# Merging the even layer's norm, projection, convolution and state space scan into lanes

## The reference, cut to what matters

```
z, xbc, dt_raw, q, k, v = split_cols(h @ w_in, EVEN_SPLITS)      # 1024, 2048, 16, 1024, 1024, 1024 columns
xbc = silu(causal_depthwise_conv(xbc, conv_w, conv_b))           # 4 taps along the tokens
xs, Bs, Cs = split_cols(xbc, (1024, 512, 512))
dt = softplus(dt_raw + dt_bias);  A = -exp(A_log)
y = ssd_chunked(xs, dt, A, Bs, Cs)                               # 4 chunks of 128 tokens, 16 heads
y = rms_norm((y + xs * D_skip) * silu(z), norm_w)
y_diff = diff_attention(q, k, v, lam, subln_w, rel_bias, layer_idx)
return concatenate([y, y_diff], axis=-1) @ w_out
```

## Time and profile before

| | us |
|---|---|
| median of 3 runs | 4740.59 |
| lowest, highest | 4728.93, 4744.25 |
| the profiled execution | 4736.4 |
| its span on the core | 4734.6 |
| PE busy | 3818.8 (81%) |
| DVE busy | 1866.7 (39%) |
| ACT busy | 1363.8 (29%) |
| POOL busy | 427.2 (9%) |

### The profile page before, as it was taken

The page is one execution under the profiler, slowest core; times in us unless marked ns, Lnnn a source line. Parts: engine busy times, 40 slices in busy tenths (PEclk is TensorE's granted clock), DMA queues, the critical chain, the costliest instruction groups (busy, mean ns, idle before and its releaser), DMA issues. The chain is left out here.

```text
span 4734.6 us, 51470 instructions
## 1 busy us (share of the span) xinstructions
PE 3818.8 (81%) x19565; PEld 2909.3 (61%) x19565; DVE 1866.7 (39%) x3013; ACT 1363.8 (29%) x2134; POOL 427.2 (9%) x403
## 2 busy tenths in 40 slices
PE   4494597779998768799789888799858988879976
PEld 4374474558766645587566744687646764468764
DVE  6534424433323233323244244344335424435433
ACT  0121323332223133322242144233324213433322
POOL 0000201002000020110003200011000310001000
PEclk5596797889999977899889886899979988789988
DMA  7520030122203101213021001231113100022220
GB/s 285 185 96 1 0 107 1 71 71 71 107 36 107 36 0 54 89 54 124 32 82 42 20 1 36 71 102 67 58 46 90 33 20 1 36 89 89 71 84 27
DMA packets 201721, 306.84 MB, mean 65 GB/s; under 512 B 12213, under 2 KB 119614, under 8 KB 201278
## 3 DMA queue, kind: packets, MB, share of 16 engines
q1 hardware_dynamic: 201534, 304.25, 18.9%
HBM read 302.12 MB, written 2.11 MB: 64 GB/s over the span
## 5 line engine op out<-in xcount | busy, mean ns | idle before, releaser
L364 DVE TENSOR_TENSOR w_lo<-ring,w_hi 128x1024 fp32r<-128x1024 f32 (+1 forms) x506 | 577.9, 1149 | 1219.2 <-ACT w_hi L359 1214.7
L359 ACT ACTIVATE w_hi<-ring 128x1024 fp32r<-128x1024 f32 (+1 forms) x506 | 491.6, 975 | 1379.9 <-PE out L375 689.8
L373 PE MATMUL out<-h_lo,w_hi 128*128 128x512 f32 x1760 | 698.8, 397 | 130.3 <-DVE w_lo L364 130.3
L374 PE MATMUL out<-h_hi,w_hi 128*128 128x512 f32 x1760 | 697.1, 396 | 0.0
L375 PE MATMUL out<-h_hi,w_lo 128*128 128x512 f32 x1760 | 696.3, 396 | 0.0
L373 PE MATMUL y<-h_lo,w_hi 128*128 128x512 f32 x1248 | 500.8, 401 | 114.7 <-DVE w_lo L364 114.7
L374 PE MATMUL y<-h_hi,w_hi 128*128 128x512 f32 x1248 | 498.4, 399 | 0.0
L375 PE MATMUL y<-h_hi,w_lo 128*128 128x512 f32 x1248 | 497.9, 399 | 0.0
L373 PEld LDWEIGHTS out<-h_lo,w_hi 128*128 128x128 f32 x1760 | 334.7, 190 | 211.2 <-issue 135.4
L374 PEld LDWEIGHTS out<-h_hi,w_hi 128*128 128x128 f32 x1760 | 334.8, 190 | 75.8
L375 PEld LDWEIGHTS out<-h_hi,w_lo 128*128 128x128 f32 x1760 | 334.5, 190 | 76.2
(11 more groups left out here) (507 smaller groups left out, 5353.8 us busy)
## 6 DMA issues: line engine op xcount, KB each, us to landing
ring<-in_mlp_w SPq DMA_DIRECT2D x28, 2048.0 KB, 8.2
ring<-in_mod_w SPq DMA_DIRECT2D x24, 2048.0 KB, 8.0
ring<-in_w_up SPq DMA_DIRECT2D x40, 1024.0 KB, 7.5
ring<-in_w_in SPq DMA_DIRECT2D x22, 1024.0 KB, 5.2
ring<-in_e_w_in SPq DMA_DIRECT2D x10, 2048.0 KB, 8.3
ring<-in_w_down SPq DMA_DIRECT2D x20, 1024.0 KB, 5.0
ring<-in_o_w_in SPq DMA_DIRECT2D x6, 2048.0 KB, 8.3
ring<-in_mlp_w SPq DMA_DIRECT2D x16, 512.0 KB, 5.3
```

Of the source, the lines that this page charges most:

```text
L359: return nc.scalar.activation(hi.bitcast(F32R), x, ACT.Copy)
L364: return nc.vector.tensor_tensor(lo.bitcast(F32R), x, hi, ALU.subtract)
L373: nc.tensor.matmul(out, wh, xl, start=start, stop=False, **kw)
L374: nc.tensor.matmul(out, wh, xh, start=False, stop=False, **kw)
```

## The change

The even layer is rewritten in the second mixer's form. `norm_lane`, `Item` and `items_lane` move up in the file and are extended: a shift in the norm, items that use two weight parts, items with a function (SiLU) on the way out, items narrower than 128 columns ("few"), and a bias for the convolution's SiLU. New are `ssd_steps_lane` and `scan_lane`. `even_mixer` takes the place of `pre_norm(k, 0)`, `even_ssd` and `even_diff`:

```diff
-        relative_bias(k, a)
-        pre_norm(k, 0)
-        with k.sbuf("mixT", [P, 16, S]) as mixT:
-            even_ssd(k, a, mixT)
-            even_diff(k, a, mixT)
-            down_project(k, a["e_w_out"][0], mixT, 4, post=lambda f: k.post_gain[:, 0, f:f + 1])
+        even_mixer(k, a)
...
+            ring = r.sbuf("ring", [P, SLOTS, DT, P])
+            w_hi, w_lo = r.sbuf("w_hi", [P, DT, 4 * P]), r.sbuf("w_lo", [P, DT, 4 * P])
+            item_banks, banks = r.psum("item_banks", [P, 2, S]), r.psum("scan_banks", [P, 6, S])
+
+            BEGIN = 16.0
+            ranges = [[(col + t * P, P if n > 1 else SSD_HEADS)] for col, n in ((E_Z, 8), (E_DT, 1), (E_XBC, XBC_T), (E_Q, HEADS), (E_K, HEADS))
+                      for t in range(n)]
+            items = [Item("rows", 2 * t, 0, 2 * P, z[:, c:c + 2, t * 2 * P:(t + 1) * 2 * P], (c, c + 1), func=ACT.Silu)
+                     for t in range(4) for c in (0, 2)]
+            items += [Item("few", 8, 0, SSD_HEADS, dt_t[0:SSD_HEADS, :])]
+            items += [Item("conv", 9 + j, 0, P, xbc[:, j, :], tile=j) for j in range(XBC_T)]
+            scan_from = len(items)
+            items += [Item("feat", 25 + j, 0, P, qT[:, j, :], scale=64 ** -0.5) for j in range(HEADS)]
+            items += [Item("feat", 33 + j, 0, P, kT[:, j, :]) for j in range(HEADS)]
+            at = BEGIN
+            for m, item in enumerate(items):
+                item.begin, item.length = at, 5.6 if m < scan_from else 8.6
+                at += item.length
...
+            begin = items[scan_from].begin + 3.6
+            settle = r.lane(begin - 0.1, 0.0)
+            ROUND = 34.0
...
+        relative_bias(k, a)
+        with k.sbuf("v_rows", [P, TC, D]) as v_rows, k.sbuf("lam_cols", [P, 2]) as lam_cols:
+            neg_lam, out_gain = lam_cols[:, 0:1], lam_cols[:, 1:2]
+            project(k, [run(2, weight_tiles(w, E_V), lambda e, t, j, ps: copy_out(nc, e, v_rows[:, j, bass.ds(t * COLS, COLS)], ps), rows=True)])
+            lambda_stage(k, a, neg_lam, out_gain)
+            diff_attention(k, qT, kT, v_rows, neg_lam, out_gain, qT, 0)
+        down_project(k, a["e_w_out"][0], (xbc, qT), 4, post=lambda f: k.post_gain[:, 0, f:f + 1])
```

In the scan the weights of a chunk (`weights`, the decays inside it) are kept for two groups of heads instead of four, the 16 matmuls of L881 become four with 512 columns, the xc copy and the POOL copies of the decays go, the SiLU of z is done when z leaves PSUM, and the loop is written out:

```diff
+                nc.tensor.matmul(banks[:, 4 + g % 2, :], k.at["after"], steps[:, g % 2, :, :], start=True, stop=True).then_inc(seg_done, 1)
...
+                if c * G + g >= 2:
+                    act.wait_ge(diag_done, c * G + g - 1)
+                nc.scalar.activation(weights[:, g % 2, :, :], banks[:, 4 + g % 2, :].rearrange("p (r n) -> p r n", r=R), ACT.Exp).then_inc(exp_done, 1)
```

SBUF is needed for the region, so `band` is no longer held: `relative_bias` runs after the region, stores the band in memory and waits for that, and the odd mixer loads it again beside its table:

```diff
+            sp.wait_ge(band_out, 4)
+            sp.dma_start(k.band_rows, k.band[:, :, :]).then_inc(band_kept, 16)
+            sp.wait_ge(band_kept, 16)
...
                         sp.dma_start(table[:, :], a["ret_table"]).then_inc(table_in, 16)
-                        sp.wait_ge(table_in, 16)
+                        sp.dma_start(k.band[:, :, :], k.band_rows).then_inc(table_in, 16)
+                        sp.wait_ge(table_in, 32)
```

More of the change, by code:

```diff
@@ L632, in weight_tiles, with norm_lane @@
     return lambda t: v[:, :, bass.ds(t * COLS + col, COLS)]
-def conv_silu(k, raw, n_tiles, taps, width, tap_col, bias_col):
+def norm_lane(k, r, lane, gain, hT, log_ms, rstd, stat, shift=None):
     nc = k.nc
[L641 to L674, removed]
-                else:
-                    step = nc.scalar.activation(out, acc[:, u, :], ACT.Silu, bias=bias_col(t))
-                step.then_inc(silu_done, 1)
-            pairs(act, n_tiles, finish)
-            nc.scalar.preload_act_table_set(EXP_LN_SET)
@@ L687, in ssd_steps, with ssd_steps_lane @@
+def ssd_steps_lane(k, r, early, lane, a, decays, rows, tmp, dt_t, stat, dt_ready):
     nc = k.nc
@@ L944, in even_ssd @@
[L944 to L959 removed]
+    dt, dt_a, eacs, to_end, total = (decays[:, i, :] for i in range(5))
@@ new lines, in _ @@
+    @lane.tensor
+    def _(pe):
+        pe.wait_ge(*dt_ready)
+        for c in range(TC):
+            last = nc.tensor.transpose(stat[:, c * H:(c + 1) * H], dt_t[0:H, c * P:(c + 1) * P], k.at["ident"][0:H, 0:H])
+        last.then_inc(turn_done, 1)
+        yield 0.75
+        pe.wait_ge(step, 9)
+        for i, m in enumerate((k.at["upto"], k.at["after"], k.at["ones"])):
+            last = nc.tensor.matmul(stat[:, (i + 1) * n:(i + 2) * n], m, dt_a, start=True, stop=True)
+        last.then_inc(sum_done, 1)
@@ new lines, in _ @@
+    @lane.scalar
+    def _(act):
+        act.wait_ge(rows_in, 48)
+        nc.scalar.activation(k.ssd_d, rows[:, 2, :], ACT.Copy).then_inc(d_copied, 1)
+        nc.scalar.activation(neg[:, 0:H], rows[:, 1, :], ACT.Exp).then_inc(neg_a, 1)
+        yield 0.2
+        act.wait_ge(step, 2)
+        nc.scalar.activation(u, mag, ACT.Exp, scale=-1.0).then_inc(exp_done, 1)
+        act.wait_ge(step, 3)
+        nc.scalar.activation(mag, w1, ACT.Ln).then_inc(log_done, 1)
+        yield 0.9
+        act.wait_ge(sum_done, 1)
+        for i, out in enumerate((eacs, to_end, total)):
+            nc.scalar.activation(out, stat[:, (i + 1) * n:(i + 2) * n], ACT.Exp).then_inc(steps_ready, 1)
```

872 lines of the change are left out of this document (437 added, 435 removed).

## The result

The changed kernel took **4583.8 us** (median of 4 runs, 4574.7 to 4586.4), the kernel before, on the same chip, 4738.7 us (median of 4, 4728.9 to 4744.3). The ratio is 0.9672, with a 95% interval of 0.9650 to 0.9694: 155 us less. The forecast was 4623 us with a range from 4595 to 4660.

The account below looks back on a forecast made before the run. Outside PE-bound projections, norm, step sizes, convolution and scan leave PE idle or slow. Region 345.5 + 18.9 + 5.4 + 55.3 = 425.1 for 545.5 us: -120.4, +3 reload, -117; 4740.6 - 117 = 4623 us, range 4595 to 4660.

Parts of the forecast that it names:

- scan beside q and k: Scan with the remaining 15.5 items: 157 us of PE, 9 us idle, 2 us tail, 168 us before the barrier.
- reload of the band in the odd layer: Odd layer: the band's reload queues behind a table and is waited for, +3 us, bounds 0 and 5.4.
- everything else: SiLU of z, dropped copies of decays and quarter-size loads priced at nothing; no term for stages outside the change.
- step-size stall: Step sizes: PE waits 5 us with the sums of the decays, bounds 1 and 12 us.
- The two ends: Rivals: q and k stand behind the scan, 4668 us, chance 0.05; PE's clock falls, 4878 us, chance 0.03.
- Waits: Scan: PE idle 9 us, the second mixer's 6% share, plus 2 us for the last chunk's tail.
- PE's own work: Scan: its loads of weights, 63.61 us before, less 15.4 us of segment products, 48.2 us.
- lane changes: Scan: 0.19 us for each of 12 interruptions a chunk by the other lane, 9 us.
- The rule weighed: Scan's y chain: GpSimd slows beside DVE through shared SBUF interfaces, 1 to 18 us in all, 4641 us at worst.
- The chain rival: Scan: the chunk's chain becomes the bound, 49.6 us a chunk instead of 42, +30 us, 4653 us, chance 0.2.
- it closes better: Rival: step-size stall 1 us, no idle in the scan, shorter norm, -18 us, 4605 us, chance 0.17.
- main case: As forecast: likeliest 4623 us, within 4613 to 4635 us, PE the bound in the scan, chance 0.55.

Follow-up runs that it names:

- scan_first: The changed kernel with the q and k items placed behind the scan instead of beside it; 4634.1 us.
- y_on_dve: The changed kernel with the three GpSimd steps of the scan's y chain given to DVE; 4575.4 us.
- turn_late: The changed kernel with the eight transposes that end each chunk two groups of products later in PE's order; 4584.8 us.
- all_match: The changed kernel with weight tiles at the same place modulo 256 bytes as the activations in every stage; 4583.1 us.
- two_products: The changed kernel with one of the three products of each q and k item left out (low part of the weights); 4563.8 us.
- before_match: The kernel before with an unused 224-byte tile ahead of the weight ring in seven stages, first MLP to second MLP; 4706.5 us.
- after_mismatch: The changed kernel with an unused 32-byte tile ahead of the weight ring in seven stages, first MLP to second MLP; 4606.1 us.
- offsets: The changed kernel with another distance, modulo 256 bytes, between the starts of weight and activation tiles in each stage; 4632.5 us.

## Why the prediction was right, and where it was wrong

| term | forecast, us | measured, us |
|---|---|---|
| norm to the end of item 0 | 33 | 32.9 |
| seven rows items | 39.2 | 39.6 |
| items 8 and 9 with the step sizes | 16.2 | 17.6 |
| fifteen convolution items, start of the scan | 87.9 | 89.1 |
| scan beside q and k (with 1.2 for the barrier in the forecast) | 169.2 | 157.6 |
| relative bias and band store | 24.3 | 22.8 |
| v projection | 55.3 | 54.9 |
| reload of the band in the odd layer | +3 | +4.4 |
| everything else | 0 | -23.6 for the pitch from the first to the second MLP (traces; -27 by the medians), -4.1 in the second blocks, -1.5 in the rest of the even layer |

**Right.** *Up to the scan* the sum stands within 3 us: 179.2 for 176.3. The step-size stall was forecast at 5 us, and 17.6 us for two items of 5.6 are 6.4 us more than the items; 3.0 of them are the wait for the sums, the rest transposes, sums and a clock of 0.87. Convolution items came 5.67 us apart on average (85.1 us for 15), not 5.57: the pitch is 0.2333 us here, where the earlier trace rows gave 0.232, and the first interval is 6.67 us, because its first products (279.68 to 281.81) still start 0.43 us apart after that wait. *The two ends* (no overlap, the clock at 1.2 GHz) did not happen, and the clock stood at 0.96 or more in every chunk.

**The scan was priced too high**, by 10.4 us. Waits came out right (11 forecast, 10.4 measured), though their size was taken over from another recurrence and not worked out, which is luck in part; items too (86.3 and 86.8 at 24 x 0.2333 us). Two terms were not. The 48.2 us of PE's own work in the earlier trace rows came from a stretch with PE idle half the time at a granted clock of 0.72; beside items the same loads sum to 43.7 us, and `scan_first`, where PE is idle again, brings the high means back (223 and 297 ns for 141 and 192). And lane changes: what is left of 157.6 after waits, items, 43.7 us and 13.6 us of segment products (0.85 us each, 13.8 forecast) is 3 us for the 9 forecast. The 0.19 us of the earlier trace rows was one interruption by twelve small products, and not the price of every one. Chunks ended 41.1, 41.1 and 36.0 us apart for the forecast 42: most of the error is in the last one.

**The rule weighed** decided the right mechanism and little time. In the timeline above, DVE's product with the decays takes 1.90 us where it needs 1.22, and ends 1.1 us after GpSimd's L972 has; then the weight split (397.93) stands until GpSimd's L975 is through, and GpSimd's L977 stands until that split ends and takes 3.27 us. In `scan_first`, with DVE idle, L977 has a mean of 2341 ns, in the changed kernel 3046; DVE's L1110 has 1213 and 2078. The Trainium skill (GPSIMD Engine Reference, 1. Specifications) names contention with DVE instructions of two SBUF inputs, and (SBUF — State Buffer, SBUF: two separate sides) calls the shared ports an exclusive lock; the trace agrees with both: 3.27 - 2.34 = 0.93 us beside an overlap of 1.01, and 1.90 - 1.22 = 0.68 us beside one of 0.83. It cost 1.6 us in this chunk's chain, within the 0.2 to 4.6 that the forecast allowed. The groups by form, in `scan_first` and then in the changed kernel:

```profile
L977 POOL TENSOR_TENSOR scan_scratch<-scan_scratch,z_rows 128x1024 f32<-128x1024 f32 x4 | 9.4, 2341 | 0.3
```

```profile
L977 POOL TENSOR_TENSOR scan_scratch<-scan_scratch,z_rows 128x1024 f32<-128x1024 f32 x4 | 12.2, 3046 | 0.3
```

What the forecast missed is that the chain was close enough to the bound for the three GpSimd steps as a whole to be worth 9 us of the scan (`y_on_dve`).

**The chain rival** (0.2, 4653 us) was half right: the chain closed each chunk with a wait, as `turn_late` and `all_match` show, but at 41 us and not 49.6. The forecast treated "PE's work plus some idle" and "the chain" as two cases; `two_products` shows that they are two parts of one round: half of what was taken from PE's work came through, and the other half turned into waits for the chain. How much of a shorter chain comes through, only `y_on_dve` shows. The case "it closes better" (4605 us) was nearest in time and wrong in its reasons: waits were those of the main case, and PE's work was smaller.

**The step that failed was "everything else: 0".** The sum adds -120.4 us for the region and +3 for the reload, and takes every other stage as it was. No step of the forecast asked what happens to stages that only move in memory. The band and `far` left SBUF, which shifted the later tiles of the first blocks, and the 32 bytes of `far` brought the weights by chance to a distance of 0 modulo 256 bytes from the activations. `before_match` and `after_mismatch` put 27 us on it from both sides (23 in the traces). On the profiled runs' own scale the forecast was 4619 for 4581.4: of these 38 us, 22 lie in the stages from the first MLP to the second one, 10 in the region, above all in the scan, 4 in the second blocks and 1.5 in the rest of the even layer. The range was built from the terms of the region alone, and so the low end stood at 4595: with the tiles at the old distance (`after_mismatch`) the time is 4606, inside it and 17 us below the forecast.

**Open.** Which part of PE or SBUF makes the distance matter; whether distances below 32 bytes or the activations' own operands (high and low part, whose starts are equal here) have a say; and the 4 to 8 us by which the second blocks differ between executions.

## What to carry to other kernels

Before a change is priced by its own instructions, list the tiles that it moves: on this kernel an unused tile of 32 or 224 bytes is worth 23 to 27 us, and a comparison of two kernels whose tiles lie at different places measures that too. When two lanes share PE, take the durations of the small products from a stretch in which PE is busy, and look at the recurrence as one ring of PE's list and a chain: a wait of 2.5 us a chunk cost some 4 us with the low clock behind it, and a shorter chain removed it, where another order did not. The chain can be shortened on an engine with room: here DVE took over three GpSimd steps.

## What the chip showed that I had not expected

- A three-product multiplication of 512 columns starts every 0.2267 us when the weights' and the activations' tiles start at the same place modulo 256 bytes of a partition, and every 0.2289 to 0.2347 us at each of the seven other distances in steps of 32 bytes, at a granted clock of 1.00 (`offsets`, `before_match`, `after_mismatch`). The Trainium skill (SBUF — State Buffer, SBUF: two separate sides) says that PE never waits on anyone at SBUF; the runs that show the difference change no other engine's work, so they do not contradict that.
- GpSimd and DVE hold each other up while their instructions overlap: the mean of a GpSimd product of 128x1024 goes from 2341 to 3046 ns, that of a DVE product from 1213 to 2078 ns.
- 7.6 us of waits in three places (at most 3.0 us each) went with a granted clock of 0.97 over a stretch of 157.6 us, and without them it was 1.00 (`y_on_dve`): 4.7 us of PE's busy time.
